# SSD block: masked matrices times dt·x, each product split into two halves of the array's columns

## The chip, the cores and the metric

The kernel runs on one core of a Trainium2 chip. Its time is the device time of one execution in microseconds (us). Before the change, three runs gave 2334.3, 2338.1 and 2340.8 us; the median is 2338.1 us. TensorE (PE in the profile) multiplies matrices, VectorE (DVE), ScalarE (ACT) and GpSimd (POOL) work element by element, SyncE (SP) issues most of the DMA transfers.

## The reference, cut to what matters

The reference is one layer of a hybrid model: a token mixer (a gated DeltaNet and a bidirectional Mamba-2 SSD side by side), then a hierarchical mixture of experts. The change lies in the SSD, in the product that gives the part of the output that comes from within a chunk of 128 tokens:

```python
seg = acum[:, :, :, None] - acum[:, :, None, :]
decay = jnp.exp(jnp.where(incl[:, :, None, None], seg, -jnp.inf))
cb = jnp.einsum("bnigs,bnjgs->bnijg", cmr, bmr)
y_diag = jnp.einsum("bnijg,bnijgr,bnjgrp->bnigrp", cb, decay, dtr[..., None] * xr)
```

For each head, a 128 x 128 matrix (`cb` times the decays, zero on one side of the diagonal) multiplies a 128 x 64 matrix, dt times x. There are 32 heads in 4 groups of 8, and 640 tokens (128 context and 512 latent ones) in 5 chunks. Everything is done twice, forwards and backwards. All numbers are float32.

## The kernel before, in words

The program is a row of blocks: position and modulation, the SSD (`ssd`, from line 1329), the DeltaNet, the merge of both, the experts, the last sum. Each block gives every engine its own list of instructions; the engines run them in order and wait for one another by semaphores (`wait_ge`). Nothing is reordered by a planner: what stands in the code is the order.

In the SSD block, the loop `for g in range(SG)` goes over the 4 groups. In a group, TensorE first projects the tokens (`proj`, lines 1433 and 1435), turns them (`turn`, L1453), and then goes over the 5 tiles of 128 tokens, `t` = 0 to 4. A tile has two steps `u` = 2t (forwards) and 2t + 1 (backwards), and each step is one call of `apply(g, u)` (L1477): 8 products, one for a head. The masked matrix `M[:, u % 2, h, :]` is the weights that are loaded into the array (128 rows by 128 columns), `dtx`, 64 columns wide, streams through it, and the result goes into 64 columns of the PSUM bank `Y`.

Around the two calls in a tile stand, in this order: `zproj` (L1488, 128 x 512 each) for the next tile's gate; `seg` (L1467), which has 24 rows alone and uses only a strip of the array's rows; from t = 1 on `states` (L1499) and `yoff` (L1509), the part that comes from earlier chunks; `cbs` (L1459), the C·B matrix of tile t + 2. At t = 4, `sums` (L1443) for the next group stands between the two calls: its weights are 32 columns wide, and four of them lie side by side in the array.

VectorE makes what `apply` reads. `decayed` (L1781) masks and scales `M`, `scaled` (L1788) makes `dtx`. Its `chain` (L1797 to L1809) waits for both products of `yoff` and adds them up; then `keep_y` (L1816) adds bank `Y`, `mask` (L1775) takes the result of `cbs`, and `decayed` and `scaled` prepare step 2t + 2. `cbs` waits for that `decayed` (semaphore `s_M`), and `apply(g, 2t + 2)` for that `scaled` (`s_dtx`). ScalarE makes the decays (`decay`, L1635), keeps turned tiles, and computes the gate's tanh.

Of the kernel before, what the change touches and what calls it, by code (L numbers as in the profile page):

```python
# [14 lines left out]
P = 128  # L15
# [6 lines left out]
SH, SP_, SG, SN = 32, 64, 4, 128  # L22
# [1306 lines left out]
def ssd(nc, sb, sem, bank, cst, C, cols, small, hT, ST, cwT, vecT, half, shared, first_in, yT, w_in, ssd_d, state_ssd, new_ssd):  # L1329

    own = ExitStack()
    with own:
# [25 lines left out]
        dtx = flat_xT[:, 0:2 * GW].rearrange("p (d n) -> p d n", d=2)  # L1358
# [7 lines left out]
        M = S("M", [P, 2, HG, P])  # L1366
# [17 lines left out]
        SEG, CB, Y, Z, STB, YOFF = 0, 2, 3, 4, 5, 6  # L1384
        hv = lambda ap: ap.rearrange("p (h e) -> p h e", e=SP_)

        with nc.Block() as block:
# [41 lines left out]
            def _(pe):  # L1429
# [40 lines left out]
                def apply(g, u):  # L1470
                    t, d = u // 2, u % 2
                    pe.wait_ge(s["s_dtx"], 10 * g + u + 1)
                    pe.wait_ge(s["s_M"], 10 * g + u + 1)
                    if d == 0 and t > 0:
                        pe.wait_ge(s["s_ykept"], 5 * g + t)
                    for h in range(HG):
                        last = pe.matmul(bank[Y][:, h * SP_:(h + 1) * SP_], M[:, u % 2, h, :], dtx[:, d, h * SP_:(h + 1) * SP_],  # L1477
                                         start=(d == 0 and h == 0), stop=(d == 1), skip_group_check=True)
                    last.then_inc(s["s_y"], 1)

                def zproj(g, t, ks):
# [33 lines left out]
                for g in range(SG):  # L1515
# [26 lines left out]
                    for d in range(2):  # L1542
                        for q in range(NQ):
                            last = pe.transpose(bank[YOFF + d][:, q * P:(q + 1) * P], srow[:, d, q, :], C(C_ID))
                    last.then_inc(s["s_initturn"], 1)

                    for t in range(NT):
                        apply(g, 2 * t)
                        if t < NT - 1:
                            zproj(g, t + 1, range(0, 4))  # L1550
                            seg(g, 2 * t + 2)
                        elif g < SG - 1:
                            pe.wait_ge(s["s_dec"], 10 * g + 10)
                            sums(g + 1)
                        if t == 0:
                            pe.wait_ge(s["s_init"], g + 1)
                            pe.wait_ge(s["s_xe"], 4 * g + 1)
                            for d in range(2):
                                for q in range(NQ):
                                    last = pe.matmul(bank[YOFF + d][:, q * P:(q + 1) * P], xe[:, 0, d, q * P:(q + 1) * P], Bt[:, 0, :], start=True, stop=True)  # L1560
                            last.then_inc(s["s_out"], 1)
                        if 1 <= t < NT - 1:
                            states(g, t, 0)
                        if t > 0:
                            yoff(g, t)
                        apply(g, 2 * t + 1)
                        if t < NT - 1:
                            zproj(g, t + 1, range(4, 6))
                            if t > 0:
                                states(g, t, 1)  # L1570
                            zproj(g, t + 1, range(6, KD))
                            seg(g, 2 * t + 3)
                        if t + 2 < NT:
                            cbs(g, t + 2)
# [7 lines left out]
                    for t in range(NT):  # L1582
# [3 lines left out]
                        for q in range(NQ):  # L1586
                            to = bank[q][:, t * P:(t + 1) * P] if t < 4 else bank[4][:, q * P:(q + 1) * P]
                            last = pe.transpose(to, ysum[:, t, q * P:(q + 1) * P], C(C_ID))
# [1183 lines left out]
```

## Time and profile before

| | |
|---|---|
| median of three runs | 2338.1 us |
| the profiled execution | 2336.3 us, its span 2334.2 us |
| TensorE busy, share of the span | 2110.1 us, 90% |
| VectorE, ScalarE, GpSimd busy | 995.9, 540.4, 276.2 us |
| mean granted TensorE clock | 0.954 of full speed |

A float32 product shows as two passes in the profile, each with one weight load (LDWEIGHTS, engine PEld) and one matmul (MATMUL, engine PE); so a call of `apply` is 16 passes. "128\*128 128x64 f32" means weights of 128 rows by 128 columns, and 128 rows by 64 columns that stream through. A matmul's shown time runs from its issue to the end of the drain, so neighbours overlap; how far apart they start tells what each costs. A timeline row gives the start, the length, the engine, the line, the operation and tiles, and how many instructions are merged in it; what stands in square brackets is the engine's idle time before the row and what ended it. A row of waits gives the sum, how often, and the longest. A row of windows gives the length of the stretch, then for each engine the busy time, and at its end the granted clock, the DMA share and the rate.

### The profile page before, as it was taken

To read this page: it belongs to the slowest core of one execution; us is meant where nothing else is said; L and a number is where in the kernel's file an instruction comes from. 1 tells how busy PE (TensorE), PEld (TensorE's weight loads), DVE (VectorE), ACT (ScalarE), POOL (GpSimd) and SP (SyncE) were. 2 spreads that over 40 slices of the span, in tenths; PEclk is the share of its full clock that TensorE was granted. 3 is DMA by queue.
4 is the path that set the end of the run, shared out by engine and by line. 5 is a ranking of instruction groups with operands and counts; after the bars stand their busy time and mean duration, and the time that the engine had idled before them with its cause. 6 is when DMAs were issued, how large, how long until landed. Compare 5 with 4: busy or idle time off the path is not lost. (4 is left out here: it accounts for less than half of the span.)

```text
span 2334.2 us, 25709 instructions
## 1 busy us (share of the span) xinstructions
PE 2110.1 (90%) x10098; PEld 1314.7 (56%) x10098; DVE 995.9 (43%) x1920; ACT 540.4 (23%) x1283; POOL 276.2 (12%) x325
## 2 busy tenths in 40 slices
PE   3799999999968999999999998999999794898985
PEld 1555555555545777877777777455555444443432
DVE  4456546465545555555555554000000086222224
ACT  1322323223212434334334344000000000111111
POOL 0020020200210111111021120000000000321102
PEclk9899999999978999999999999999999895899998
DMA  8121111210011101100101010893241544699973
GB/s 300 52 63 46 27 37 46 64 46 23 23 50 29 28 14 41 28 15 28 33 23 28 15 37 8 266 288 108 81 135 28 225 167 198 202 402 412 396 304 140
DMA packets 177799, 259.97 MB, mean 111 GB/s; under 512 B 14759, under 2 KB 146664, under 8 KB 163344
## 3 DMA queue, kind: packets, MB, share of 16 engines
q1 hardware_dynamic: 151096, 219.04, 27.3%
q10 hardware_dynamic: 18488, 23.54, 3.5%
q0 software_dynamic: 8096, 15.75, 1.9%
q8 instruction: 80, 1.31, 0.2%
q14 instruction: 39, 0.32, 0.0%
HBM read 231.78 MB, written 39.10 MB: 116 GB/s over the span
## 5 line engine op out<-in xcount | busy, mean ns | idle before, releaser
L673 PE MATMUL bank<-hT,shared 128*128 128x512 f32 x384 | 180.6, 600 | 8.0 <-DMA shared<-in_w_in_dram 8.0
L1433 PE MATMUL bank<-hT,shared 128*128 128x512 f32 x384 | 169.3, 594 | 2.6 <-DVE xT L1806 1.8
L2405 PE MATMUL bank<-ring,xgT 128*64 128x512 f32 (+1 forms) x416 | 150.6, 632 | 15.4 <-DMA ring<-in_w_exp_up_dram 11.3
L1488 PE MATMUL bank<-wz,hT 128*128 128x512 f32 x320 | 153.0, 616 | 0.0
L1201 DVE TENSOR_TENSOR X<-bank,negm 128x512 f32<-128x512 f32 x144 | 81.8, 598 | 133.9 <-PE bank L743 133.8
L751 PE MATMUL bank<-DT,X 128*128 128x128 f32 x960 | 126.9, 276 | 4.0 <-DVE X L1201 4.0
L743 PE MATMUL bank<-D_,MT 128*128 128x128 f32 x960 | 127.3, 283 | 0.0
L1987 DVE SCALAR_TENSOR_TENSOR prod<-gth,bank 128x512 f32<-128x512 f32 x16 | 11.0, 687 | 272.6 <-PE bank L1957 272.6
L751 PEld LDWEIGHTS bank<-DT,X 128*128 128x128 f32 x960 | 118.1, 192 | 14.8 <-issue 8.4
L743 PEld LDWEIGHTS bank<-D_,MT 128*128 128x128 f32 x960 | 118.7, 198 | 0.9
L1433 PEld LDWEIGHTS bank<-hT,shared 128*128 128x128 f32 x384 | 71.1, 190 | 84.3 <-issue 84.1
L2405 PEld LDWEIGHTS bank<-ring,xgT 128*64 128x64 f32 (+1 forms) x416 | 56.9, 166 | 99.6 <-issue 99.6
L1957 PE MATMUL bank<-yT,wm 128*128 128x512 f32 x256 | 111.2, 592 | 0.0
L970 ACT COPY D_<-bank 128x512 f32<-128x512 f32 x144 | 73.5, 516 | 158.3 <-PE bank L760 158.2
L673 PEld LDWEIGHTS bank<-hT,shared 128*128 128x128 f32 x384 | 67.9, 193 | 63.3 <-issue 55.1
L975 ACT COPY DT<-bank 128x512 f32<-128x512 f32 x144 | 74.1, 522 | 113.9 <-PE bank L751 111.8
L1957 PE MATMUL bank<-hT,wm 128*128 128x512 f32 x224 | 98.0, 595 | 0.0
L1488 PEld LDWEIGHTS bank<-wz,hT 128*128 128x128 f32 x320 | 59.7, 197 | 63.5 <-issue 63.5
L1477 PEld LDWEIGHTS bank<-xT,M 128*128 128x128 f32 x640 | 77.9, 196 | 19.0 <-DVE xT L1788 11.0
L1756 DVE SCALAR_TENSOR_TENSOR sroom<-spadded,scw,sroom 128x644 f32<-128x644 f32 x96 | 85.4, 890 | 3.4
L2141 PE MATMUL bank<-ring,shared 128*128 128x512 f32 x160 | 72.9, 617 | 15.4 <-DMA ring<-in_w_o_dram 15.4
L1142 DVE SCALAR_TENSOR_TENSOR conv<-padded,cw,conv 128x644 f32<-128x644 f32 x96 | 85.3, 889 | 3.1
(409 smaller groups left out, 3453.5 us busy)
## 6 DMA issues: line engine op xcount, KB each, us to landing
shared<-in_w_in_dram SPq DMA_DIRECT2D x62, 512.0 KB, 5.7
ring<-in_w_exp_gate_dram SPq DMA_DIRECT2D x26, 1024.0 KB, 11.9
ring<-in_w_exp_up_dram SPq DMA_DIRECT2D x26, 1024.0 KB, 19.4
ring<-in_w_exp_down_dram SPq DMA_DIRECT2D x26, 1024.0 KB, 15.4
aw<-in_w_ada_dram SPq DMA_DIRECT2D x8, 2048.0 KB, 9.9
yd<-mzero ACTq DMA_DIRECT2D x1, 16128.0 KB, 106.8
aw<-in_w_ada_dram SPq DMA_DIRECT2D x8, 1024.0 KB, 21.5
wz<-in_w_in_dram SPq DMA_DIRECT2D x4, 2048.0 KB, 7.8
```

The lines of the kernel that those rows point to most:

```text
L673: pe.matmul(bank[LATB[j]][:, :], wof(j)[:, k, :], hT[:, k, SEQ:T], start=(k == 0), stop=(k == KD - 1), skip_group_check=True)
L743: last = pe.matmul(xdv(g)[:, u * P:(u + 1) * P], MT[:, u0 + u, :], D_[:, u0 + u, :], start=True, stop=True, skip_group_check=True)
L751: last = pe.matmul(dtv(g)[:, u * P:(u + 1) * P], X[:, u0 + u, :], DT[:, u0 + u, :], start=(g == 2), stop=(g == 2 or l == LEVELS - 1), skip ...
L975: act.copy(DT[:, u0:u0 + m, :], tiles4(dtv(g))).then_inc(s["g_DTkept"], 1)
L1142: ins = STT(out=to, in0=x[:, k:k + CW], scalar=cw[:, k, j:j + 1], in1=to, op0=ALU.mult, op1=ALU.add)
L1201: ins = TT(out=X[:, u0:u0 + m, :], in0=tiles4(xdv(g)), in1=mask, op=ALU.mult)
L1433: pe.matmul(bank[a][:, :], wn(n)[:, k, :], hT[:, k, SEQ:T], start=(k == 0), stop=(k == KD - 1))
L1477: last = pe.matmul(bank[Y][:, h * SP_:(h + 1) * SP_], M[:, u % 2, h, :], dtx[:, d, h * SP_:(h + 1) * SP_], start=(d == 0 and h == 0), stop ...
L1488: last = pe.matmul(bank[Z][:, :], hT[:, k, t * P:(t + 1) * P], wz[:, k, :], start=(k == 0), stop=(k == KD - 1), skip_group_check=True)
L1756: ins = STT(out=c3, in0=padded[:, n % 3, k:k + CW], scalar=cw[:, k, n:n + 1], in1=c3, op0=ALU.mult, op1=ALU.add)
L1957: last = pe.matmul(bank[j][:, :], W(at + k), src[:, k, SEQ:T], start=(k == 0), stop=(k == kk - 1))
L2405: last = pe.matmul(bank[2 + slot][at, :], xgT[:, slot, k, at], wgu[w][:, k, :, :], start=(k == 0), stop=(k == KD - 1))
```

## The change

In `apply`, each product becomes two. The weights are taken 64 columns at a time: columns 0 to 63 of the masked matrix give rows 0 to 63 of the result, columns 64 to 127 give rows 64 to 127. Both halves use all 128 rows of the array, and each reads the same 64 columns of `dtx`. Waits, banks and the order of the steps stay as they are.

```diff
                     for h in range(HG):
-                        last = pe.matmul(bank[Y][:, h * SP_:(h + 1) * SP_], M[:, u % 2, h, :], dtx[:, d, h * SP_:(h + 1) * SP_],
-                                         start=(d == 0 and h == 0), stop=(d == 1), skip_group_check=True)
+                        for c in (slice(0, P // 2), slice(P // 2, P)):
+                            last = pe.matmul(bank[Y][c, h * SP_:(h + 1) * SP_], M[:, u % 2, h, c], dtx[:, d, h * SP_:(h + 1) * SP_],
+                                             start=(d == 0 and h == 0), stop=(d == 1), skip_group_check=True)
                     last.then_inc(s["s_y"], 1)
```

The line numbers after the changed lines grow by one (L1477 becomes L1478, L1488 becomes L1489, and so on).

TensorE's order from the start of the first tile of a group (t = 0), before; the last column is the shape of the result, partitions by columns, and `xT` is the storage that holds `dtx` here:

```order
L1544 MATMUL bank<-cst,srow 128x128 x8
L1477 MATMUL bank<-xT,M 128x64 x8
L1488 MATMUL bank<-wz,hT 128x512 x4
L1467 MATMUL bank<-uptoT,fromT 128x512 x2
L1560 MATMUL bank<-Bt,sroom 128x128 x8
L1477 MATMUL bank<-xT,M 128x64 x8
L1488 MATMUL bank<-wz,hT 128x512 x4
```

and the same place after the change:

```order
L1545 MATMUL bank<-cst,srow 128x128 x8
L1478 MATMUL bank<-xT,M 64x64 x16
L1489 MATMUL bank<-wz,hT 128x512 x4
L1467 MATMUL bank<-uptoT,fromT 128x512 x2
L1561 MATMUL bank<-Bt,sroom 128x128 x8
L1478 MATMUL bank<-xT,M 64x64 x16
L1489 MATMUL bank<-wz,hT 128x512 x4
```

Nothing has moved; in the two rows of `apply`, 8 products of 128 rows have become 16 of 64. The row ahead of each and the row behind it use the array's full width.

TensorE's order in the last tile of a group (t = 4), from the `seg` ahead of it, before:

```order
L1467 MATMUL bank<-uptoT,fromT 128x512 x2
L1477 MATMUL bank<-xT,M 128x64 x8
L1443 MATMUL bank<-cst,wide 32x128 x20
L1509 MATMUL bank<-sroom,CT 128x512 x2
L1477 MATMUL bank<-xT,M 128x64 x8
L1433 MATMUL bank<-hT,shared 128x512 x8
```

and after the change:

```order
L1467 MATMUL bank<-uptoT,fromT 128x512 x2
L1478 MATMUL bank<-xT,M 64x64 x16
L1443 MATMUL bank<-cst,wide 32x128 x20
L1510 MATMUL bank<-sroom,CT 128x512 x2
L1478 MATMUL bank<-xT,M 64x64 x16
L1433 MATMUL bank<-hT,shared 128x512 x8
```

Here the first `apply` stands between two rows that use the array in strips already, `seg` and `sums`.

## Rows read from the trace of the kernel before

**Rows 1.** The page: busy time, share and count of TensorE's matmuls and loads.

```profile
PE 2110.1 (90%) x10098; PEld 1314.7 (56%) x10098; DVE 995.9 (43%) x1920; ACT 540.4 (23%) x1283; POOL 276.2 (12%) x325
```

**Rows 2.** Line 1477: durations in ns (least/median/most), first and last start.

```profile
L1477 PE MATMUL bank<-xT,M x640: 219/275/422, 152.2 to 667.2; 128*128 128x64 f32 x160
```

**Rows 3.** TensorE's waits in the stretch 150 to 670 us.

```profile
PE bank L1459 <- DVE M L1781: 5.8, 8, 0.7
PE bank L1477 <- DVE xT L1788: 5.3, 4, 1.3
```

**Rows 4.** Timeline of TensorE, group 0, tiles 1 and 2.

```profile
174.53 1.88 PE L1509 MATMUL bank<-sroom,CT 128*128 128x512 f32 x4
176.24 1.89 PE L1477 MATMUL bank<-xT,M 128*128 128x64 f32 x16
177.97 1.94 PE L1488 MATMUL bank<-wz,hT 128*128 128x512 f32 x4
...
184.28 0.49 PE L1459 MATMUL bank<-CT,BT 128*128 128x128 f32 x2 [0.73 <-DVE M L1781]
184.88 2.00 PE L1477 MATMUL bank<-xT,M 128*128 128x64 f32 x16
186.71 3.65 PE L1488 MATMUL bank<-wz,hT 128*128 128x512 f32 x8
190.30 1.13 PE L1467 MATMUL bank<-uptoT,fromT 24*128 24x512 f32 x4
```

**Rows 5.** Timeline of VectorE, group 0, tiles 1 and 2.

```profile
176.44 1.29 DVE L1802 TENSOR_TENSOR sroom<-sroom,scur 128x512 f32<-128x512 f32 x2 [6.52 <-PE bank L1509]
...
184.15 0.68 DVE L1788 TENSOR_TENSOR xT<-xt,scur 128x512 f32<-128x512 f32 x1
184.75 0.67 DVE L1792 SCALAR_TENSOR_TENSOR yT<-szth,bank 128x512 f32<-128x512 f32 x1
...
194.23 1.29 DVE L1802 TENSOR_TENSOR sroom<-sroom,scur 128x512 f32<-128x512 f32 x2 [7.07 <-PE bank L1509]
...
201.92 0.68 DVE L1788 TENSOR_TENSOR xT<-xt,scur 128x512 f32<-128x512 f32 x1
```

**Rows 6.** The experts' products with 64 weight columns, two halves: first loads; nine pairs.

```profile
L2405 PEld LDWEIGHTS bank<-ring,xgT x4: 132/134/136, 2050.9 to 2051.0; 128*64 128x64 f32 x4
...
2050.92 0.20 PEld L2405 LDWEIGHTS bank<-ring,xgT 128*64 128x64 f32 x4 [0.76 <-issue]
...
2050.92 4.08 PE L2405 MATMUL bank<-ring,xgT 128*64 128x512 f32 x18
```

**Rows 7.** Timeline of the loads at the start of `sums`, group 0.

```profile
102.07 0.16 PEld L1443 LDWEIGHTS bank<-cst,wide 128*32 128x32 f32 x8
```

**Rows 8.** Timeline of TensorE, group 0, tile 4.

```profile
222.13 2.00 PE L1477 MATMUL bank<-xT,M 128*128 128x64 f32 x16 [1.32 <-DVE xT L1788]
224.06 1.30 PE L1443 MATMUL bank<-cst,wide 128*32 128x128 f32 x40
225.28 1.98 PE L1509 MATMUL bank<-sroom,CT 128*128 128x512 f32 x4
```

**Rows 9.** Windows of the SSD block with the clock at half.

```profile
204.50:207.90 3.40, 3.40 (x6) 1.42 (x6) 0.77 (x2) 0.00 (x0) 0.00 (x0) 0.50 0.00 0
...
330.80:337.60 6.80, 6.80 (x20) 4.53 (x20) 1.88 (x3) 0.00 (x0) 0.00 (x0) 0.50 0.00 0
...
515.10:518.50 3.40, 3.40 (x43) 2.50 (x43) 0.32 (x1) 1.03 (x2) 0.00 (x0) 0.50 1.06 380
...
624.30:627.70 3.40, 3.40 (x10) 2.16 (x10) 1.01 (x2) 0.00 (x0) 0.00 (x0) 0.51 0.00 0
...
661.90:665.30 3.40, 3.40 (x8) 1.83 (x7) 0.64 (x2) 0.00 (x0) 0.00 (x0) 0.50 0.00 0
```

**Rows 10.** Timeline of TensorE, group 0, tile 3.

```profile
204.49 5.35 PE L1488 MATMUL bank<-wz,hT 128*128 128x512 f32 x8
209.77 1.13 PE L1467 MATMUL bank<-uptoT,fromT 24*128 24x512 f32 x4
```

## The prediction

> **What bounds the kernel now.** I began with the page's busy times: TensorE is busy for 90% of the span [rows 1], so a change of its work can count, if it stands where TensorE is not waiting. The changed line has 640 passes between 152 and 667 us [rows 2], all in the SSD block. Next I read the waits of that stretch: TensorE waits for VectorE's `M` 8 times in front of `cbs` and for `dtx` 4 times in front of `apply` [rows 3], which is once in each of the tiles t = 2, 3 and 4 of the four groups. The timelines say who sets the pace there. VectorE starts the chain of tile 1 at 176.44, when `yoff` is done, and ends `scaled` at 184.15 + 0.68 = 184.83; TensorE starts `apply` at 184.88. In tile 2 it is 194.23 and 202.60 [rows 4, 5]. So a turn of the loop is 8.4 us of VectorE from `yoff` to `scaled`, and then TensorE's work from `apply(2t + 2)` to the next `yoff`. The backward `apply` of tiles 1 to 3 lies beside VectorE's chain: after it, TensorE waits for 0.73 us in front of `cbs` and 0.11 in front of `apply` [rows 4] anyway.
>
> On the path are therefore, in a group, six of ten calls: `apply(0)`, `(1)`, `(2)`, where TensorE never waits; `(4)`, `(6)` and `(8)`, which start when VectorE is done. Off it are `(3)`, `(5)`, `(7)` and `(9)`; behind the last, the next group's projection waits for VectorE too.
>
> **What a call costs today.** `apply` starts at 176.24 and the next line's first matmul at 177.97, but that one still waits for its weights: its four matmuls take 1.94 instead of the 1.88 of `yoff`'s four [rows 4]. So a call is 177.97 + 0.06 − 176.24 = 1.79 us, 0.112 a pass. The matmul doesn't set that: four passes of 512 columns from 174.53 to 176.24 are 0.43 each, so 64 columns stream in 0.054 us [rows 4]. The load of 128 weight columns does.
>
> **The change part by part.** The 16 passes become 32, with weights of 64 columns. Nothing of the kind with a short stream is in the trace, but two shapes stand on either side. The experts' product has the same two halves: its 18 matmuls of 512 columns take 4.08 us, 9 × 0.43 and a drain, so two halves run in the time of one. Four loads of 64 columns, two for each half, take 0.20 us together where one shows 0.134 [rows 6], so the fourth starts 0.06 after the first: the halves' loads run side by side, and the second load of a half starts a bit under 0.06 after its first. In `sums`, eight loads of 32 columns are through in 0.16 us [rows 7]; one after another, at 0.112 for 128 columns, they would take 0.22.
>
> So a pair of halves (one pass of each) should cost the longer of a matmul, 0.054, and a load, 0.06. The ends are 0.054, if the load hides fully, and 0.112, if the halves' loads share one way in and together cost what a full one costs today. I take 0.06, the row of the same shape. Sixteen pairs are 0.96 us.
>
> Each switch between the full width and strips adds something. From one full-width line to another, TensorE's next line starts 0.17 before the shown end (174.53 + 1.88 against 176.24); from `zproj` to `seg` only 0.06 to 0.07 before it (186.71 + 3.65 against 190.30) [rows 4]: 0.10 of drain. And the first load is not hidden: `yoff` after `sums` takes 1.98, without a switch 1.88 [rows 8, 4], so 0.10 for 128 columns; for 64 columns the nine pairs above leave 4.08 − 8 × 0.43 − 0.59 = 0.05. Going in costs 0.10 + 0.05, coming out 0.10 + 0.10.
>
> - `apply(0)`, `(1)`, `(2)`, between work of full width: 0.15 + 0.96 + 0.20 = 1.31 instead of 1.79, a gain of 0.48 each.
> - `apply(4)`, `(6)`: TensorE has waited, so the drain going in is free, and the first load is open before and after: 0.05 + 0.96 + 0.20 = 1.21 instead of 0.10 + 1.79 = 1.89; 0.68 each.
> - `apply(8)`: as these, but `sums` behind it makes a switch today too: 0.05 + 0.96 + 0.10 = 1.11 instead of 1.93 (222.13 to 224.06, [rows 8]); 0.82, and 0.68 in the last group, which has no `sums`.
>
> A group gives 3 × 0.48 + 2 × 0.68 + 0.82 = 3.62, the last 3.48; together 3 × 3.62 + 3.48 = 14.3 us. The four calls off the path get 0.48 shorter too and give nothing: the wait in front of `cbs` grows from 0.73 to about 1.2. What is late next is VectorE's chain, of which nothing changes. `zproj` behind `apply(4)` needs VectorE's gate of the tile before, which is there at 184.75 + 0.67 = 185.42 [rows 5], 1.3 before that line's start at 186.71 and so by more than the gain of 0.68. No wait is added, no DMA is issued earlier or later than its place in the order, and the 16 extra passes of a call are 64 small instructions in a microsecond, fewer than the 80 of `sums` (40 passes in 1.30 us, [rows 8]). The blocks behind the SSD start that much earlier and are as long as before.
>
> With 0.054 for a pair the sum is 24 × 16 × 0.006 = 2.3 more, 16.6; with 0.112 it is 24 × 16 × 0.052 = 20.0 less, a loss of 5.7.
>
> **The clock.** The granted clock falls from full (2.4 GHz) to half (1.2 GHz) behind some of these waits: at 204.5, 515.1, 624.3 and 661.9 for 3.4 us, at 330.8 for 6.8 [rows 9], each within 3 us of the end of such a wait, so behind five of the twelve. The price of the first: eight matmuls of `zproj` take 209.77 − 204.49 = 5.28 up to the next line, and in the tile before 3.59 [rows 10, 4], so 1.7 us. The waits get longer by 0.5, the work on both sides of them stays what it is, and I expect about as many falls: plus or minus two, 3.4 us.
>
> **The rivals.** Their times stand against the median of the runs, 2338.1, which is 1.8 above the profiled execution's 2336.3.
> 1. The halves' loads don't run side by side when the stream is short, and a pair costs 0.112: 5.7 us more, 2344. For it: no row has this shape. Against it: rows 6 and 7.
> 2. Longer waits in front of `cbs` and of `apply(8)` let the clock fall more often. If seven more waits are followed by a fall, at 1.7 each, that is 11.9 of the 14.3 given back, 2336; at the price of the 330.80 fall, twice as long and so about 3.4, it is 23.8, and the kernel is slower, 2348. It decides from nine short falls on, or five long ones. Against it: 7 of 12 such waits are not followed by a fall today.
> 3. The halves don't overlap at all: each pass loads, then streams, 0.06 + 0.054 = 0.114, and 32 of them are 3.65 us. A call between other work is then 3.65 + 0.35 − 1.79 = 2.2 longer, a waiting one about 2.0, and the calls off the path overrun their wait by 0.9 to 1.4; that is 4 × (6.6 + 4.0 + 1.9 + 3.7) = 65 us, 2403. Against it: eight matmuls of `zproj`, each with a load of its own, take 0.43 apiece in rows 4, so loads hide behind matmuls in all rows of the array, and rows 6 has halves side by side. The Trainium skill has it as a rule, in "TensorE: Matmul & The Clock Gate", "The mechanism": a weight load overlaps with a running matmul only where it goes to another group of rows, and matmuls keep their order. By that rule this time would come out; the trace doesn't agree with it, by the 0.43 just named.
> 4. The calls off the path count as well, 16 × 0.48 = 7.7 more: 2316. Against it: the 0.73 of waiting that rows 4 shows.
>
> **How the numbers follow.** The sum puts the profiled execution at 2336.3 − 14.3 = 2322.0, and the median of runs, 1.8 higher, at 2324. My forecast has a chance of 0.80 and its own range of 2316 to 2331 (a pair between 0.054 and 0.07, the clock, the scatter of the runs before, 2334 to 2341). Rival 1 has 0.07, rival 2 0.06, rival 3 0.02, rival 4 0.05. The range of 2315 to 2336 leaves out rivals 1 and 3, half of 2 and the edges of the rest. A measurement of this kernel tells about 0.3% or 7 us from no change. Faster by more than that: the forecast but for 0.02, rival 4 and a sixth of rival 2, 0.84; within it 0.11 (most of rival 1, half of rival 2, the forecast's edge); slower 0.05.
>
> **What would show it.** In the profile after, `apply` should take about 1.0 us from its first to its last start, with the next line 1.3 us after the call began where no wait is in it; the loads should show near 135 ns; the waits in front of `cbs` should be about 1.2 us in tiles 2 and 3; VectorE's 8.4 us should stay. If a pair takes 0.11, rival 1 holds; if the line is as short as I say and the time is not, the count of half-clock stretches decides. I am wrong if `apply(4)` gets shorter and the loop from `yoff` to `yoff` does not.

## Result and the profile after

The changed kernel takes 2322.6 us (median of four runs, 2320.89 to 2324.0), the kernel before 2337.1 beside it (four runs): 14.5 us less; the ratio of the mean times is 0.9937, with a 95% interval of [0.9919, 0.9954]. The profiled execution's span is 2322.1 us, before 2334.2. TensorE's busy time fell, and its instructions grew by 640, to 10738 [rows 1]:

```profile
PE 2086.3 (90%) x10738; PEld 1283.1 (55%) x10738; DVE 1003.4 (43%) x1920; ACT 540.4 (23%) x1283; POOL 279.5 (12%) x325
```

VectorE has the same 1920 instructions as before and is busy for 1003.4 − 995.9 = 7.5 us longer. That is the first sign of something the prediction doesn't have. The changed line, by its source (count, least/median/most ns, stretch, shape, passes):

```profile
L1478 PEld LDWEIGHTS bank<-xT,M x1280: 132/138/231, 153.3 to 654.3; 128*64 128x64 f32 x183
L1478 PE MATMUL bank<-xT,M x1280: 222/222/369, 153.3 to 654.3; 128*64 128x64 f32 x183
```

The passes have doubled [rows 2] and every one uses 64 columns; the loads show 138 ns, where about 135 were forecast. Now TensorE's timeline in tiles 1 and 2 of group 0, to be read against [rows 4] (start, length, line, shape, count, wait ahead of it):

```profile
173.98 1.88 PE L1510 MATMUL bank<-sroom,CT 128*128 128x512 f32 x4
175.79 1.15 PE L1478 MATMUL bank<-xT,M 128*64 128x64 f32 x32
176.87 1.98 PE L1489 MATMUL bank<-wz,hT 128*128 128x512 f32 x4
...
184.42 0.49 PE L1459 MATMUL bank<-CT,BT 128*128 128x128 f32 x2 [1.93 <-DVE M L1782]
185.02 1.69 PE L1478 MATMUL bank<-xT,M 128*64 128x64 f32 x32
186.64 4.76 PE L1489 MATMUL bank<-wz,hT 128*128 128x512 f32 x8
191.33 1.13 PE L1467 MATMUL bank<-uptoT,fromT 24*128 24x512 f32 x4
```

Where nothing waits, 32 passes take 1.15 us where 16 took 1.89. The account of a call can be checked term by term. `yoff` to `apply` is 175.79 − 173.98 = 1.81, before 1.71: the drain of 0.10 on the way in. The call is 176.87 − 175.79 = 1.08, and `zproj` behind it takes 1.98 instead of 1.88: the open load of 0.10 on the way out. The sum is 1.28 instead of 1.79. With 0.05 for the first load and 0.10 for the second drain, the sixteen pairs have 0.93, 0.058 each.

The wait in front of `cbs` is 1.93, not the 1.2 that was forecast, and the clock was at half behind it (`apply` 1.69, `zproj` 4.76). In tile 3, whose backward call and wait follow the same plan, the wait is 1.23, as forecast:

```profile
203.09 0.49 PE L1459 MATMUL bank<-CT,BT 128*128 128x128 f32 x2 [1.23 <-DVE M L1782]
```

The same in the view of waits over the SSD block, against [rows 3] (idle us, times, longest):

```profile
PE bank L1459 <- DVE M L1782: 12.6, 8, 1.9
...
PE bank L1478 <- DVE xT L1789: 7.3, 4, 1.8
```

What is 0.7 us late in tile 2 stands in VectorE's timeline of tile 1, and beside it GpSimd's first product there (the last row):

```profile
175.90 1.30 DVE L1803 TENSOR_TENSOR sroom<-sroom,scur 128x512 f32<-128x512 f32 x2 [6.01 <-PE bank L1510]
...
178.55 0.69 DVE L1810 TENSOR_TENSOR ysum<-ysum,xT 128x512 f32<-128x512 f32 x1
...
180.00 1.38 DVE L1810 TENSOR_TENSOR ysum<-ysum,xT 128x512 f32<-128x512 f32 x1
...
184.28 0.68 DVE L1789 TENSOR_TENSOR xT<-xt,scur 128x512 f32<-128x512 f32 x1
...
179.80 1.04 POOL L1705 TENSOR_TENSOR sroom<-xt,dter 128x512 f32<-128x512 f32 x1 [13.93 <-PE bank L1500]
```

and the same two operations of the kernel before:

```profile
180.55 0.69 DVE L1809 TENSOR_TENSOR ysum<-ysum,xT 128x512 f32<-128x512 f32 x1
...
180.85 1.29 POOL L1704 TENSOR_TENSOR sroom<-xt,dter 128x512 f32<-128x512 f32 x1 [16.95 <-PE bank L1499]
```

From the start of this chain to the end of `scaled` VectorE needs 184.28 + 0.68 − 175.90 = 9.06 us, where 8.4 was forecast to stay. The second addition into `ysum` takes 1.38 instead of 0.69 when GpSimd's product began 0.20 before it, and it ends 0.54 behind that product (181.38 against 180.84). Before the change the addition began 0.30 ahead, and there the product is the longer one, 1.29 instead of 1.04. GpSimd waits there for `states(1,1)`, which stands behind the backward call `apply(3)`: that call has become shorter, so GpSimd starts 1.05 earlier, while VectorE's addition is only 0.55 earlier. This occurs once in each group, four times in all, in this place: 2.8 of VectorE's 7.5 us.

The Trainium skill has the rule, in "SBUF — State Buffer", "Who interferes with whom": a VectorE instruction with two inputs in SBUF contends with a GpSimd instruction that reads SBUF, and the order of issue decides who is blocked. The trace agrees on the order (the addition 1.38 behind, 0.69 ahead).

Another 3.4 of the 7.5 us are the same collision in a place where it costs nothing: `scaled` of step 2, beside an earlier product of GpSimd. Here are both after the change, and `scaled` before it:

```profile
164.89 1.52 DVE L1789 TENSOR_TENSOR xT<-xt,scur 128x512 f32<-128x512 f32 x1
...
163.85 2.02 POOL L1705 TENSOR_TENSOR sroom<-xt,dter 128x512 f32<-128x512 f32 x1
```

```profile
164.90 0.68 DVE L1788 TENSOR_TENSOR xT<-xt,scur 128x512 f32<-128x512 f32 x1
```

It ends at 166.41, and TensorE starts `apply(2)` at 167.25. The kernel before has such a long `scaled` too, in step 1 of every group.

The clock, in windows (length, TensorE's busy time, loads, VectorE, ScalarE, GpSimd; the third number from the end is the granted clock):

```profile
185.40:188.80 3.40, 3.40 (x31) 2.25 (x26) 1.90 (x3) 0.00 (x0) 0.00 (x0) 0.50 0.03 5
...
362.90:366.30 3.40, 3.40 (x41) 2.21 (x31) 0.89 (x2) 1.50 (x3) 0.00 (x0) 0.50 1.06 382
...
468.70:475.50 6.80, 6.36 (x39) 3.96 (x40) 3.32 (x5) 0.00 (x0) 0.00 (x0) 0.50 0.00 0
...
489.20:492.60 3.40, 3.40 (x36) 2.54 (x36) 3.03 (x8) 0.00 (x0) 0.00 (x0) 0.50 0.02 5
...
615.50:618.90 3.40, 3.40 (x14) 1.74 (x11) 1.40 (x2) 0.00 (x0) 0.00 (x0) 0.50 0.00 0
```

Up to the last `apply` these are five stretches at half clock, 20.4 us, where [rows 9] have five with 20.4 us.

To part work from clock I use one sum for all kernels, the **plain turn**: for each of the ten stretches of a group, from the first matmul of one `apply` to that of the next (the last one to the next line), the shortest of the four groups, added up. In the last group other work stands behind `apply(8)` and `apply(9)`, so for these two it is the shortest of the first three. What the stretches took above their shortest is the **cost of the falls**. Before, the plain turn is 75.66 us and the falls cost 8.4 in 38 stretches. The fall at 661.9 [rows 9] is in the last group's `apply(8)`, which takes 5.29 where it takes 3.61 without a fall (experiment 9): 1.7 more, 10.1 together. After, the plain turn is 72.48 and the falls cost 9.0, none of them in that stretch. Four groups give 4 × 3.18, less 0.14 in the last, which has no `sums`: 12.6 us off, and 1.0 by falls, together 13.6. Outside the stretches 1.6 is given back: the first `apply` starts 1.1 later, with 3.4 us more at half clock ahead of it, the three projections between groups take 0.1 more each (the open load behind `apply(9)`), and the rest behind the SSD block 0.2. That leaves 12.0 of the 12.1 by which the spans differ. The medians of the runs differ by 14.5.

One run of all those below, in experiment 7, took 7003.7 us, three times the others of its kernel, and nothing on record shows why; no ratio or range below has it.

### The profile page after: what moved, and what is told of

The parts are those of the page before. It is cut to its first block and busy times, and to the rows that moved or that the text cites. A ratio compares the mean times of both kernels' runs of the same rounds, so it can differ in the third digit from the quotient of the medians.

```text
span 2322.1 us, 26989 instructions
## 1 busy us (share of the span) xinstructions
PE 2086.3 (90%) x10738; PEld 1283.1 (55%) x10738; DVE 1003.4 (43%) x1920; ACT 540.4 (23%) x1283; POOL 279.5 (12%) x325
## 5 line engine op out<-in xcount | busy, mean ns | idle before, releaser
L1489 PE MATMUL bank<-wz,hT 128*128 128x512 f32 x320 | 154.5, 621 | 0.0
L1489 PEld LDWEIGHTS bank<-wz,hT 128*128 128x128 f32 x320 | 59.7, 197 | 65.6 <-issue 63.2
L1958 PEld LDWEIGHTS bank<-yT,wm 128*128 128x128 f32 x256 | 48.6, 190 | 61.2 <-issue 61.2
## 6 DMA issues: line engine op xcount, KB each, us to landing
ring<-in_w_exp_gate_dram SPq DMA_DIRECT2D x26, 1024.0 KB, 12.1
```

The lines of the kernel that those rows point to most:

```text
L1489: last = pe.matmul(bank[Z][:, :], hT[:, k, t * P:(t + 1) * P], wz[:, k, :], start=(k == 0), stop=(k == KD - 1), skip_group_check=True)
L1958: last = pe.matmul(bank[j][:, :], W(at + k), src[:, k, SEQ:T], start=(k == 0), stop=(k == kk - 1))
```

## The experiments

The changed kernel is the base unless another is named; each figure is a median beside runs of the kernel before on the same chip, then the ratio of the means and its interval. Falls are counted up to the last `apply`.

**1. The changed kernel again**, to see how firm time and falls are.

> The changed kernel once more, beside the next three on the same chip. Every theory: 2322.6 us as before, within the scatter of its runs (2320.9 to 2324.0). In its profile, the theory of the collision expects in each of the four groups one addition of VectorE to ysum in the chain of tile 1 that takes 1.4 us instead of 0.7, while GpSimd multiplies for the last states; if that was chance, it is gone.

Measured: 2320.2 (2319.7 to 2325.2) against 2337.9, 0.9929 [0.9915, 0.9943]. The plain turn is 72.47, the addition is long in all four groups again; the clock falls four times, in part at other places, which costs 6.3 us. The work repeats to 0.01 us, the falls don't.

**2. Halves only in the calls off the path; 3. only in those on it.**

```diff
-for c in (slice(0, P // 2), slice(P // 2, P)):
+for c in ((slice(0, P // 2), slice(P // 2, P)) if u in (3, 5, 7, 9) else (slice(0, P),)):
```

with `if u not in (3, 5, 7, 9)` for the third.

> Only the backward calls of tiles 1 to 4 (u = 3, 5, 7, 9) are split, the other six of a group stay whole. Theory A (these four lie beside VectorE's chain): no gain, the wait in front of cbs grows from 0.73 to about 1.2 us; and since the split call of tile 1 lets the states of tile 1 and so GpSimd's last multiplications start 0.6 us earlier, the collision with VectorE costs 0.7 us in each group: 2337.1 + 2.8 = 2340 us. Rival (every call counts alike): 16 calls of 0.65 us less, 2327 us. Rival without the collision: 2337 us.

> Only the calls on the path (u = 0, 1, 2, 4, 6, 8) are split, the backward calls of tiles 1 to 4 stay whole. Theory A with the collision: the whole gain, and the 2.8 us of the collision are saved, since GpSimd's last multiplications start as late as they did before the change: 2322.6 - 2.8 = 2320 us; the addition to ysum takes 0.7 us in all groups and from yoff to apply(4) VectorE needs 8.5 us again instead of 9.2. Theory A without the collision: 2322.6 us, the same as all split. Rival (every call counts alike): 60% of the gain, 2328 us.

Measured: 2349.9, 1.0052 [1.0038, 1.0065], and 2312.6, 0.9895 [0.9880, 0.9910]. Halves in the four calls off the path don't just bring nothing, they cost 12 us; without them the change is better by 8 (2312.6 against 2320.2 in experiment 1, on the same chip). The difference shows in the work and in the clock. The plain turn of the third is 71.78, 0.70 under the changed kernel's, and its addition stands ahead of GpSimd again:

```profile
179.60 0.69 DVE L1810 TENSOR_TENSOR ysum<-ysum,xT 128x512 f32<-128x512 f32 x1
...
179.90 2.29 POOL L1705 TENSOR_TENSOR sroom<-xt,dter 128x512 f32<-128x512 f32 x2 [14.44 <-PE bank L1500]
```

Its clock falls once, which costs 1.6 us; that of the second falls eight times and is at half for 44.2 us, twice as long as before. There the longer wait is followed by a call with whole weights, at half clock:

```profile
480.31 0.49 PE L1459 MATMUL bank<-CT,BT 128*128 128x128 f32 x2 [1.93 <-DVE M L1782]
480.91 3.27 PE L1478 MATMUL bank<-xT,M 128*128 128x64 f32 x16
483.97 5.77 PE L1489 MATMUL bank<-wz,hT 128*128 128x512 f32 x8
```

**4. GpSimd's products later**, behind VectorE's `M` of step 5 (tile 2, backwards), so that they can't stand beside the additions:

```diff
                         if p == 3:
                             pool.wait_ge(s["s_st"], 6 * g + 2)
+                            pool.wait_ge(s["s_M"], 10 * g + 6)
```

> All calls are split, and GpSimd's last multiplications of a group (line 1705, for the states of tile 3) wait for VectorE's M of step 5, so they come after the chain of tile 1 and not beside it. If the collision is the cause of the longer chain: the addition to ysum takes 0.7 us again, from yoff to apply(4) 8.5 us instead of 9.2, and 2322.6 - 2.8 = 2320 us. If VectorE's addition is longer for another reason (a wait that the profile doesn't show, the shorter call on TensorE): it stays at 1.4, and 2322.6 us.

Measured: 2311.1 (2306.6 to 2317.8), 0.9885 [0.9865, 0.9904]: 9 us better than the changed kernel (experiment 1), the plain turn 71.77. The rows of tile 1, GpSimd's start, and the waits in front of `cbs`, none over 1.2 now:

```profile
180.16 0.69 DVE L1811 TENSOR_TENSOR ysum<-ysum,xT 128x512 f32<-128x512 f32 x1
...
186.31 2.36 POOL L1706 TENSOR_TENSOR sroom<-xt,dter 128x512 f32<-128x512 f32 x2 [20.28 <-DVE M L1783]
```

```profile
PE bank L1459 <- DVE M L1783: 9.9, 8, 1.2
```

With all calls in halves and the products out of the way, the addition is 0.69 again, and VectorE's 8.4 us from `yoff` to `scaled` are back in tiles 1 to 3 of every group: the collision is shown as the cause of the 0.69. It is worth 4 × 0.69 = 2.8 in the plain turn; the other 6 are falls, one in the profile (1.6 us) where the two profiles of the changed kernel have five (9.0) and four (6.3). The traces say where: in each of the two of the changed kernel a fall follows the wait of tile 2 in three of the four groups, in those of experiments 3 and 4 in none.

**5. The halves one after the other**: all sixteen passes of one half, then those of the other, so that neighbours in the queue need the same columns.

```diff
-for h in range(HG):
-    for c in (slice(0, P // 2), slice(P // 2, P)):
+for c in (slice(0, P // 2), slice(P // 2, P)):
+    for h in range(HG):
```

> All calls are split as in the changed kernel, but the eight lower halves of a call come first and the eight upper ones after them, so that neighbours in the queue use the same half of the array. Same instructions, same sizes. Theory S (the gain comes from two halves running side by side, and only neighbours in the queue do): 32 passes at 0.058 us are 1.87 us, with switches 2.2 instead of the 1.79 of a whole call; on the path 4 x (3 x 0.43 + 2 x 0.23 + 0.1) = 7 us more than the kernel before, 2344 us. Rival (a 64 column load is cheap enough by itself, or the engine looks far enough ahead to pair the halves anyway): 1.27 us for a call and 2323 us, as the changed kernel.

Measured: 2329.4 (2326.2 to 2332.0) against 2338.8, 0.9954 [0.9937, 0.9970].

```profile
163.23 1.90 PE L1478 MATMUL bank<-xT,M 128*64 128x64 f32 x32
165.06 3.70 PE L1489 MATMUL bank<-wz,hT 128*128 128x512 f32 x8
```

The call is 165.06 − 163.23 = 1.83 instead of 1.08. In the trace single passes start 0.058 apart, where in the changed kernel pairs do: what the change gains is that two neighbours take different halves. The time was missed. The plain turn is 76.27, 0.6 above before, where 1.75 was expected. In the middle of a call, where one half gives way to the other, three passes start 0.003 to 0.006 behind another one, which makes each call some 0.18 shorter than 32 × 0.058; on the six calls of the path that is the 1.1 that is missing. So the rival in the expectation was right for a few passes. The row of windows counts the passes early in the call and in its middle:

```profile
163.40:163.75 0.35, 0.35 (x9) 0.35 (x9) 1.00 0.00 0
163.88:164.23 0.35, 0.35 (x13) 0.35 (x12) 1.00 0.00 0
```

And the clock never falls, so that the kernel is faster than before with more plain work. Its longer calls fill part of the waits: those in front of `cbs` are 0.5 at most, 3.9 us together.

**6. Quarters**, 32 columns each; **7. quarters with GpSimd's products later** (edit of 4).

```diff
-for c in (slice(0, P // 2), slice(P // 2, P)):
+for c in (slice(32 * n, 32 * n + 32) for n in range(4)):
```

> Each product is split into four quarters of 32 weight columns instead of two halves; 64 passes in a call. Theory S (side by side, and the cost is the longer of load and stream): a load of 32 columns takes less than the stream of 64, so four passes cost the stream, 0.056 us instead of the 0.058 of a pair, and the first load is 0.03 shorter: 24 x (16 x 0.002 + 0.03) = 1.5 us less than the changed kernel, 2321 us. Rival (a pass has a price of its own, in the queue or in the load): at the 0.029 us that a pass of a half costs today, 64 passes are 1.87 us and the kernel is at about 2342 us.

> The two edits that helped by themselves, together: quarters of 32 weight columns, and GpSimd's last multiplications of a group behind VectorE's M of step 5. If their gains are independent: the addition to ysum takes 0.7 us, a call 1.03 us from start to start, without falls of the clock a group is 0.5 us shorter than with halves and the late multiplications; 2311.1 - 2 = 2309 us, with at most two falls in the SSD block. Rival (the quarters' gain of e5_quarters was fewer falls alone): 2311 us.

Measured: 2316.5, 0.9904 [0.9887, 0.9920], and 2311.2 (four runs; 2312.8 with the fifth), 0.9887 [0.9871, 0.9903].

```profile
326.08 0.49 PE L1459 MATMUL bank<-CT,BT 128*128 128x128 f32 x2 [1.93 <-DVE M L1782]
326.68 1.10 PE L1478 MATMUL bank<-xT,M 128*32 128x64 f32 x64
327.71 3.70 PE L1489 MATMUL bank<-wz,hT 128*128 128x512 f32 x8
```

64 passes take 1.10 us where 32 took 1.15: four passes start 0.056 after four, close to the 0.054 of a stream, so the loads are all but hidden. The plain turns are 71.98 and 71.34: quarters bring 0.43 to 0.50 a group, and the collision (again 1.93 in front of `cbs`) costs 0.64. The seventh is no better than the fourth in time (2311.1); in its profile the falls cost 3.1 instead of 1.6.

**8. The second with GpSimd's products later.** If the collision made the second kernel slow, this should mend it.

> Only the backward calls of tiles 1 to 4 are split, as in e1_off, and GpSimd's last multiplications come late. This takes the collision out of e1_off. If its slowness was the collision and the longer wait that it makes in tile 2 (1.9 us) in front of a whole call: waits of 1.2 us, no long addition, as much work on the path as in the kernel before (0.1 us a call more for the switches), and some falls of the clock more than there, since the waits are 1.2 instead of 0.7: 2340 us, 10 below e1_off. If the split calls off the path are slow by themselves: as e1_off, 2350 us.

Measured: 2356.3 (2351.7 to 2359.1), 1.0072 [1.0059, 1.0086]. A miss.

```profile
486.40 0.49 PE L1459 MATMUL bank<-CT,BT 128*128 128x128 f32 x2 [1.24 <-DVE M L1783]
487.00 2.80 PE L1478 MATMUL bank<-xT,M 128*128 128x64 f32 x16
489.60 6.26 PE L1489 MATMUL bank<-wz,hT 128*128 128x512 f32 x8
```

The wait is 1.24 instead of 1.93, all additions take 0.69, and yet the clock falls eleven times, 71.4 us at half. So the collision is not what makes the second kernel slow. Three pairs of kernels show what goes with the falls. In each, the waits in front of `cbs` are the same, and the kernels differ only in the six calls on the path, whole in one and halved in the other:

| waits in front of `cbs` (8), us | calls on the path whole | calls on the path halved |
|---|---|---|
| 5.8 | before: 5 falls | 3: 1 fall |
| 12.6 | 2: 8 falls | changed: 5 and 4 falls |
| 9.9 | 8: 11 falls | 4: 1 fall |

The rows of waits of experiments 3, 2 and 8, in this order (the other three stand in [rows 3], in the result and in experiment 4):

```profile
PE bank L1459 <- DVE M L1782: 5.8, 8, 0.7
...
PE bank L1459 <- DVE M L1782: 12.6, 8, 1.9
...
PE bank L1459 <- DVE M L1783: 9.9, 8, 1.2
```

Behind the same waits, whole calls go with more falls. All runs agree by their granted clocks, not the profiled ones alone: 0.950 to 0.955 against 0.956 to 0.959, 0.948 or 0.949 against 0.952 to 0.955, 0.944 to 0.946 against 0.954 to 0.960. Why the eighth kernel, with the shorter waits, has more falls than the second stays open, and no run fills the waits of these two.

**9. The waits filled, in the kernel before**: behind `seg` of tiles 1 to 3, one or two products of `B` with `C` into a bank that is free, which nobody reads.

```diff
+if t > 0:
+    pe.wait_ge(s["s_stkept"], 6 * g + 2 * t)
+for _ in range((0, 1, 1, 2)[t]):
+    pe.matmul(bank[STB][:, 0:2 * P], BT[:, t, :], CT[:, 0:2, :].rearrange("p t n -> p (t n)"), start=True, stop=True)
```

> The kernel before, whole calls, with products put in that nobody reads: one of 256 columns (2 passes, 0.43 us) behind the last seg of tiles 1 and 2, two behind that of tile 3, into the bank of the states, which is free then. They fill most of the wait in front of cbs and of apply(8). Theory C (the clock falls because TensorE waits and then trickles): 6 falls of the clock in the SSD block become at most 2, and the kernel gets faster by the 8.4 us that the falls behind the waits cost in the profile of before: 2330 us, though it does more. Rival (the falls have nothing to do with these waits, or the work added costs): 2338 us or more.

Measured: 2324.4 (2321.2 to 2327.5) against 2338.9, 0.9943 [0.9931, 0.9956]. Added work that nobody reads makes the kernel before as fast as the change does. The unread product (L1576) stands where the 0.73 of waiting was, and the rest starts when it did, by the 0.28 later at which this group begins:

```profile
182.70 1.13 PE L1467 MATMUL bank<-uptoT,fromT 24*128 24x512 f32 x4
183.75 0.70 PE L1576 MATMUL bank<-CT,BT 128*128 128x256 f32 x2
184.56 0.49 PE L1459 MATMUL bank<-CT,BT 128*128 128x128 f32 x2
185.16 2.00 PE L1477 MATMUL bank<-xT,M 128*128 128x64 f32 x16
```

The plain turn is 75.67, before 75.66, and no stretch has a fall. Over these 515 us of the block the granted clock is 1.00, before 0.98 (windows; first before, then this one):

```profile
150.00:665.00 515.00, 500.30 (x2162) 283.95 (x2162) 290.65 (x477) 144.75 (x302) 66.35 (x64) 0.98 0.13 37
```

```profile
150.00:665.00 515.00, 502.29 (x2212) 285.53 (x2210) 297.28 (x487) 148.22 (x312) 67.64 (x66) 1.00 0.13 37
```

**10. The waits filled in the changed kernel**, with (0, 2, 2, 3) products; **11. all together**: quarters, GpSimd's products later, waits filled.

> The changed kernel (all calls in halves, collision and all) with such products in its waits: two, two and three behind the last seg of tiles 1, 2 and 3. Theory C: the falls go (9.0 us in the profile of the changed kernel, 6.3 in its repeat), the collision's 0.7 us in each group stays: 2321.5 - 7 = 2314 us, with four additions of 1.4 us still there; it stays some 3 us above e3_late, which has neither. If the falls don't come from the waits: 2322 us.

> The three edits that helped, together: quarters, GpSimd's last multiplications late, and two, two and three products that nobody reads in TensorE's waits of tiles 1, 2 and 3. If each does what it did alone: a call 1.03 us, no long addition, no fall of the clock in the SSD block but the one at its end; 3.1 us of falls less than the profile of e6_both, 2312.8 - 3 = 2310 us. Rival (the added products hold up what comes behind the waits when these are shorter): 2313 us or more.

Measured: 2312.7, 0.9894 [0.9878, 0.9910], with no fall and the plain turn of 72.48 that the changed kernel has; and 2306.2 (2304.5 to 2310.6) against 2338.4, 0.9868 [0.9850, 0.9887], with no fall and 71.35. The last beats both kernels: the changed one by some 15 us.

| kernel | ratio to before | plain turn, us | cost of the falls, us | long additions into `ysum` |
|---|---|---|---|---|
| before | 1 | 75.66 | 10.1 | 0 |
| changed | 0.9937 | 72.48 | 9.0 | 4 |
| 1 again | 0.9929 | 72.47 | 6.3 | 4 |
| 3 on the path | 0.9895 | 71.78 | 1.6 | 0 |
| 4 products later | 0.9885 | 71.77 | 1.6 | 0 |
| 5 one after the other | 0.9954 | 76.27 | 0 | 0 |
| 6 quarters | 0.9904 | 71.98 | 3.9 | 4 |
| 7 quarters, later | 0.9887 | 71.34 | 3.1 | 0 |
| 9 before, filled | 0.9943 | 75.67 | 0 | 0 |
| 10 changed, filled | 0.9894 | 72.48 | 0 | 4 |
| 11 all | 0.9868 | 71.35 | 0 | 0 |

(The second and the eighth have falls in every group, so their shortest stretches are no plain turn.)

## Why the prediction was right, and where it wasn't

The time, the sign and the mechanism came as forecast: 2322.6, where 2324 was forecast. That it came so close is in part luck: a work gain 0.8 above the forecast, a collision of 2.8 that the forecast doesn't have, falls that cost 1.0 less, and medians that moved 2.4 us more than the profiled spans. By its steps:

- **The pair of halves at 0.06**: 0.058 from the call's rows. Rival 1 (0.112) is out, and so is rival 3: it has a pass of a half at 0.114, and this one takes 0.058 even when its neighbour uses the same columns (experiment 5), 0.029 when it doesn't. The rule that it names, in the Trainium skill's "TensorE: Matmul & The Clock Gate", "The mechanism", lets a load overlap with a running matmul only where it goes to another group of rows; these passes use all 128 rows, and the trace doesn't agree with it, by the same numbers.
- **The switches**: 0.10 in, 0.10 for the load on the way out, as read from [rows 4, 8].
- **The gains on the path**, from the plain turn's stretches: `apply(0)`, `(1)`, `(2)` 0.51 each, forecast 0.48; from the start of `apply(3)` to that of `apply(5)`, which holds `apply(4)`, 0.70 without the collision, forecast 0.68, and the same for `apply(6)`; `apply(8)` 0.85, forecast 0.82. In tile 4 it starts behind a longer wait (1.83, before 1.32) and `sums` comes 1.08 later, before 1.93:

```profile
220.77 1.15 PE L1478 MATMUL bank<-xT,M 128*64 128x64 f32 x32 [1.83 <-DVE xT L1789]
221.85 1.30 PE L1443 MATMUL bank<-cst,wide 128*32 128x128 f32 x40
```

With 0.10 more at the group's end that makes 3.89 a group (75.66 − 71.77 in experiment 4); the next group's projection, 0.10 longer, gives that 0.10 back. Forecast were 3.62.
- **The calls off the path bring nothing**: right; with halves there alone the kernel gains nothing, and rival 4 is out. That they can do harm, ahead of whole calls, was not seen.
- **"VectorE's chain, of which nothing changes"** is the step that failed. I followed whom TensorE's shorter call releases on VectorE, not on GpSimd: `states(1,1)` comes earlier, GpSimd's products with it, and VectorE's addition beside them lasts 0.69 longer, once a group. That took 2.8 of a gain in work that was 15.1 without it, and left 12.3 where 14.3 was forecast (both with the projections between the groups). In the chain's own terms, the 8.4 us from `yoff` to `scaled` that should stay became 9.1 in tile 1 of each group and stayed 8.4 in tiles 2 and 3.
- **The clock**: as many falls as before, five, was right for the profiled execution, but by two things that oppose each other, neither of which I had: behind the same waits halved calls go with fewer falls than whole ones (the three pairs in experiment 8), and the 1.93 us wait that the collision makes goes with more (five and four falls with it, one without, experiment 4). Rival 2, more falls through longer waits, is not what the change did; with whole calls behind the longer waits the falls did become more (second and eighth kernel, 1.0052 and 1.0072).

The medians moved 2.4 us more than the profiled spans. Single profiles don't settle this, as falls change from run to run (five, then four, in the same kernel). The size of experiment 9 is open in part, too: its median gained 14.5, with an interval of 10 to 16, and its profiled span 15.0. Of these, 10.0 lie in the forty stretches, which is what the falls of the profile of before cost; 5.2 lie behind the SSD block, where the code is the same and the thirteen profiles take from 1653 to 1659 us. That the usual run of before has more falls than the profiled one would fit its clock (0.951 to 0.954 in the runs of before on that chip, 0.954 in the profile), but no profile shows it.

## What to carry to other kernels

Short products whose weight loads set the pace can be split by columns, with neighbours in the queue in different halves; the price is the switches on both sides, so split where the call is on the path and leave the others whole. When an instruction gets shorter, follow everyone it releases, the engine you don't count on too: an earlier start there can land on a neighbour's operation. And before working on a stage with short waits, look whether the clock falls behind them; here products that nobody reads, put into the waits, brought 10 us in the profiled stretches and 14.5 in the medians, about as much as the change.

## What the runs showed of the hardware

- An addition of 512 float32 columns on VectorE, both inputs in SBUF, takes 0.69 us, and 1.38 where a multiplication of 1.04 us on GpSimd started 0.20 us ahead of it; with the addition 0.30 ahead, it takes 0.69 and GpSimd's multiplication 1.29. A multiplication of the same size on VectorE takes 0.68, and 1.52 where one of 2.02 us on GpSimd started 1.04 ahead. Both end 0.54 us behind GpSimd's.
- Loads and streams of the two column halves go side by side: 0.058 us for a pair of passes of 64 weight columns with 64 streamed columns, and 0.058 for one pass if both neighbours use the same half; quarters bring the 64 passes of a call to 1.10 us.
- A switch between weights of 128 and of 64 columns costs 0.10 us of drain each way, and 0.05 (64 columns) to 0.10 us (128) for a first load that nothing hides: 0.10 on the way in and 0.10 on the way out stand in the rows of a call.
- The clock fell to half behind some of the waits of 0.7 to 1.9 us, at places that differ from run to run: four to five times in the changed kernel, eleven times in the eighth, never where the waits were filled. Behind the same waits it fell more often where whole calls followed than where halved ones did. Which of the waits it follows stays open.
